# Attention groups in the order of dilation 1, 16, 4, loads in order of need, and the gate projection behind q

## What is computed

```python
ada = silu(c) @ w_ada + b_ada                      # shift, scale, gate: 3 x 1024
h = rms_norm(x, norm_g) * (1 + scale) + shift
z = h @ w_in                                       # 8704 columns
# branch A: three groups of 8 heads, each with its own q, k, v (512 columns each)
for g, (window, dilation) in enumerate(((128, 1), (512, 4), (2048, 16))):
    q = partial_rope(rms_norm(z_q[g])); k = partial_rope(rms_norm(z_k[g]))
    # a token attends to t - j * dilation, j = 0 .. 128, within its residue class
    o[g], denominator[g] = dilated_window_attention(q, k, z_v[g], window, dilation)
attn = sum of o[g], weighted by the softmax denominators over the groups
y_a = attn * silu(z_gate_a)
# branch B: chunked spatial gating
u, v = split(gelu(z_b)); v = layer_norm(v)
y_b = u * (tril(w_spatial) @ v + b_spatial) * silu(z_gate_b)
merged = sigmoid(z_mA) * (y_a @ w_branch_a) + sigmoid(z_mB) * (y_b @ w_branch_b)
out = x + gate * (merged @ w_out)
```

## Time and profile before

| | |
|---|---|
| median of 6 runs | 810.89 us (809.9 to 884.0) |
| the profiled execution, its own time | 810.75 us |
| span from its first to its last instruction, slowest core | 809.2 us |
| spans of the 8 cores | 805.3 to 809.2 us |
| PE busy | 741.5 us (92%) |
| DVE busy | 457.6 us (57%) |
| ACT busy | 375.4 us (46%) |
| POOL busy | 272.5 us (34%) |
| moved by DMA | 61.98 MB |

### The profile page before, as it was taken

One profiled execution on the slowest core, in us unless ns is written; L12 is line 12 of the kernel. 1 busy time (PEld: TensorE's weight loads), 2 busy tenths in 40 slices (PEclk: granted clock), 3 DMA queues, 4 the chain that ended last, 5 costly groups with the idle time before them and its releaser, 6 DMA issues.

```text
span 809.2 us, 14709 instructions; the slowest of 8 cores (805.3 to 809.2 us)
## 1 busy us (share of the span) xinstructions
PE 741.5 (92%) x4936; PEld 369.9 (46%) x4936; DVE 457.6 (57%) x730; ACT 375.4 (46%) x659; POOL 272.5 (34%) x332
## 2 busy tenths in 40 slices
PE   4776799999999899999888899989998999999996
PEld 0223455555666565454444444444443444444442
DVE  5335578876677577776666676566664222333333
ACT  2205678688766566676666655534221111111110
POOL 0002122433453434332122300367732333333334
PEclk9889899999999999999999999999999999999999
DMA  8992320360653000200000050709594122131314
GB/s 253 290 238 61 86 86 2 53 105 2 106 73 33 14 1 2 52 2 2 1 1 2 6 99 1 130 2 143 105 256 122 53 68 90 53 103 53 104 53 157
DMA packets 23481, 61.98 MB, mean 77 GB/s; under 512 B 5616, under 2 KB 12016, under 8 KB 20976
## 3 DMA queue, kind: packets, MB, share of 16 engines
q0 software_dynamic: 13472, 22.40, 18.2%
q1 hardware_dynamic: 7488, 30.26, 12.1%
q10 hardware_dynamic: 2448, 8.39, 2.6%
HBM read 75.05 MB, written 8.39 MB: 103 GB/s over the span
## 4 chain that ended last, share of the span: by engine, by line
PE 70%; DVE 9%; ACT 6%; issue 5%; DMA 4%; POOL 3%; SPq 1%; DVEq 0%; ACTq 0%; POOLq 0%
PE ps L236 61%; DVE arena L245 9%; ACT arena L245 6%; DMA arena<-w_ada 3%; POOL arena L245 3%; PE ps L368 2%; PE ps L548 2%; PE ps L581 2%; PE ps L508 2%; PE ps L585 1%; SPq L248 1%; PE ps L344 1%; PE ps L895 1%; DMA arena<-wsp 0%; DVEq L1043 0%
## 5 line engine op out<-in xcount | busy, mean ns | idle before, releaser
L236 PE MATMUL ps<-arena 128*128 128x512 bf16 x2692 | 615.7, 384 | 25.1 <-ACT arena L245 15.4
L236 PEld LDWEIGHTS ps<-arena 128*128 128x128 bf16 x2692 | 278.3, 108 | 315.8 <-issue 47.8
L245 POOL TENSOR_TENSOR arena<-arena 128x128 bf16<-128x128 f32 (+5 forms) x298 | 252.7, 856 | 441.7 <-DVE arena L245 421.5
L245 ACT ACTIVATE arena<-ps 128x1024 bf16<-128x1024 f32 (+2 forms) x283 | 193.9, 708 | 309.0 <-PE ps L236 216.2
L245 DVE TENSOR_TENSOR arena<-ps,arena 128x512 bf16<-128x512 f32 (+2 forms) x218 | 153.0, 734 | 90.7 <-ACT arena L245 41.3
L245 DVE SCALAR_TENSOR_TENSOR arena<-arena,ps 128x512 f32<-128x512 f32 x80 | 54.6, 686 | 119.9 <-PE ps L236 99.5
L245 DVE TENSOR_REDUCE arena<-arena 128x8 f32<-128x512 bf16 x96 | 65.8, 685 | 64.7 <-ACT arena L245 64.7
L245 ACT ACTIVATE arena<-arena 128x16 f32<-128x16 f32 (+5 forms) x185 | 77.9, 426 | 49.7 <-DVE arena L245 35.6
L245 DVE TENSOR_TENSOR arena<-arena 128x1024 bf16<-128x1024 bf16 (+5 forms) x116 | 72.5, 632 | 27.0 <-ACT arena L245 25.7
L245 ACT ACTIVATE arena<-ps,arena 128x512 bf16<-128x512 bf16 x96 | 60.9, 690 | 3.4 <-PE ps L508 3.4
L245 DVE TENSOR_SCALAR arena<-arena 128x256 bf16<-128x256 bf16 (+6 forms) x84 | 44.5, 571 | 24.7 <-ACT arena L245 17.6
(11 more groups left out here) (36 smaller groups left out, 134.8 us busy)
## 6 DMA issues: line engine op xcount, KB each, us to landing
arena<-x SPq DMA_DIRECT2D x32, 512.0 KB, 5.2
arena<-w_in POOLq DMA_DIRECT2D x16, 1024.0 KB, 14.6
out<-arena ACTq DMA_DIRECT2D x15, 512.0 KB, 4.9
arena<-w_ada SPq DMA_DIRECT2D x7, 1024.0 KB, 18.3
arena<-w_adag SPq DMA_DIRECT2D x8, 512.0 KB, 8.8
arena<-w_out POOLq DMA_DIRECT2D x2, 1024.0 KB, 29.2
arena<-w_ada SPq DMA_DIRECT2D x2, 512.0 KB, 32.9
arena<-w_in POOLq DMA_DIRECT2D x4, 256.0 KB, 9.0
```

Of the source, the lines that this page charges most:

```text
L236: ins = e.matmul(out_ap, l, r, start=(i == 0), stop=(i == n - 1))
L245: P.op(eng, lambda e: getattr(e, meth)(*a, **kw), reads=reads, writes=writes)
```

## The change

1. The groups come in the order of dilation 1, 16, 4. Each step of the first group needs one x tile of its own only, so names of scaled x (`hm`) are kept per tile, and x is scaled tile by tile and in pairs. The first group writes `acc`, now without a stride; the last, of dilation 4, adds.
2. SP loads w_ada 0, 1, 2, then x tiles 0 to 3, then w_ada 3; POOL loads Wq, Wk, Wv in halves, each gated by the landing of an earlier piece; x tiles 4 to 7 wait for Wv's first half.
3. At the start the rows, tables and x tiles come in another order; six of the eight scalings `x_mod4` stand in front of the last adaLN row. The x tiles 4 to 6 are prepared behind the q and k projections of steps 0 to 3 instead of between them.
4. `finZ` stands behind the next step's q projection, `finA` behind its k projection, `finB` behind its v projection; finB's product goes to POOL for token blocks 0 to 2.
5. The mask of the spatial weights is spread over 8 iterations.
6. `sv_mm` and `sv_y` come one step later for the first three token blocks, `gate_fin` and the outputs one merge later.

The diff, cut to its core:

```diff
+    def load_half(s, c0, h, gate):
+        P.op("pool", lambda e: e.dma_start(out=wslot[s][:, 4 * h:4 * h + 4, :], in_=win_v(c0, 512)[:, 4 * h:4 * h + 4, :]),
+             reads=[gate], writes=["ws%d" % s + "b" * h], slot="ws%d" % s + "b" * h)
...
         for c in range(4):
+            if c == 3:
+                for t in range(4):
+                    x_load(t)
...
-            if c < 2:
-                x_load(2 * c)
-                x_load(2 * c + 1)
-        dma("pool", wslot[0], win_v(1536, 512), "ws0", reads=["wada1_0"])
+        gate = "wada3_0"
+        for j in range(3):
+            for h_ in range(2):
+                load_half(j, 512 * j, h_, gate if h_ == 0 else "ws%d" % (j - 1) if j else "wada3_4")
+            gate = "ws%d" % j
...
-        dma("pool", wslot[1], win_v(2048, 512), "ws1", reads=["wada3_0"])
-        dma("pool", wslot[2], win_v(2560, 512), "ws2", reads=["wada3_6"])
...
-            x_load(t + 4, gate=["ws1"] if t >= 2 else [])
+            x_load(t + 4, gate=["ws2"])
         ada_row(0)
-        x_in(0, 3)
-        x_in(1, 4)
         ada_row(1)
         ada_col(0)
-        x_in(2, 5)
-        x_in(3, 6)
-        rot_tables(1)
+        rot_tables(0)
         ada_tr(0)
         ada_row(2)
         ada_col(1)
         rot_tables(2)
         ada_tr(1)
+        rot_tables(1)
+        for t in range(4):
+            x_in(t, 3 + t)
+        ada_col(2)
+        ada_tr(2)
+        for kc in range(6):
+            x_mod4(0, kc)
         ada_row(3)
-        ada_col(2)
-        rot_tables(0)
-        ada_tr(2)
         ada_col(3)
         ada_tr(3)
+        x_mod4(0, 6)
+        x_mod4(0, 7)
...
-        steps = [(1, r * 4 + n) for n in range(4) for r in range(4)]
+        steps = [(0, n) for n in range(16)]
         steps += [(2, r) for r in range(16)]
-        steps += [(0, n) for n in range(16)]
-        prev = [(s - 4 if s >= 4 else None) for s in range(16)] + [None] * 16 + [None] + list(range(32, 47))
+        steps += [(1, r * 4 + n) for n in range(4) for r in range(4)]
+        prev = [None] + list(range(15)) + [None] * 20 + list(range(32, 44))
...
-            X("dve", "tensor_tensor", [k0, k1], ["ya%d_%d" % (hp, tb), "ws4", "ws5"], out=y_aT[:, hp, ts_], in0=f0, in1=f1, op=ALU.mult)
+            X("dve" if tb == 3 else "pool", "tensor_tensor", [k0, k1], ["ya%d_%d" % (hp, tb), "ws4", "ws5"], out=y_aT[:, hp, ts_], in0=f0, in1=f1, op=ALU.mult)
...
             proj(it, 0)
             sumsq(it, 0)
+            if it - 1 in fin_at:
+                finZ(*fin_at[it - 1])
             if not one(b_):
                 scores(b_, 0)
                 mask(b_, 0)
-            if it - 1 in fin_at:
-                finA(*fin_at[it - 1])
-            if it + 5 < NT:
-                x_transp(it + 5, TB)
-                x_evac(it + 5, TB)
+            if it + 3 < NT:
+                x_transp(it + 3, TB)
+                x_evac(it + 3, TB)
...
             proj(it, 1)
             sumsq(it, 1)
             if it - 1 in fin_at:
-                finB(*fin_at[it - 1])
+                finA(*fin_at[it - 1])
...
-            if it in (4, 6, 8, 10):
-                x_mod(it + 4, 2)
+            if it in (4, 6, 8, 10, 12):
+                x_mod(it + 2, 2)
             proj(it, 2)
             vevac(it)
+            if it - 1 in fin_at:
+                finB(*fin_at[it - 1])
             transp(a)
-            if it in fin_at:
-                finZ(*fin_at[it])
...
-                for g_ in range(8):
-                    X("pool", "tensor_tensor", ["cst", "WsT"], ["WsT"], out=WsT[:, g_, :], in0=WsT[:, g_, :], in1=mD, op=ALU.mult)
+            if 25 <= it < 33:
+                X("pool", "tensor_tensor", ["cst", "WsT"], ["WsT"], out=WsT[:, it - 25, :], in0=WsT[:, it - 25, :], in1=mD, op=ALU.mult)
...
-            for n, ks in enumerate(((1, 2, 4, 5), (3, 5, 7, 8), (7, 9, 11, 12), (11, 13, 15, 15))):
+            for n, ks in enumerate(((1, 2, 5, 6), (3, 5, 8, 9), (7, 9, 12, 13), (11, 13, 15, 15))):
...
-                        gate_fin()
                         for t in range(4):
                             x2_load(t)
-                else:
-                    outp(8 * (tb - 1) + fc)
+                elif tb == 1:
+                    if fc == 0:
+                        gate_fin()
+                    else:
+                        outp(fc - 1)
+                        if fc == 7:
+                            outp(7)
+                elif tb == 2:
+                    outp(8 + fc)
+                elif fc > 0:
+                    outp(15 + fc)
+        outp(23)
```

More of the change, by code:

```diff
@@ L351, in x_mod4 @@
         def x_mod4(n, kc):
-            X("dve", "tensor_scalar", [B(3), B(4), B(5), B(6), "ab%d" % (kc // 2)], ["hm%d_%d" % (n, kc)],
+            X("dve", "tensor_scalar", [B(3), B(4), B(5), B(6), "ab%d" % (kc // 2)], ["hm%d_%d" % (4 * n + i_, kc) for i_ in range(4)],
               out=hT[:, kc, 0:512].rearrange("p (t w) -> p t w", t=4), in0=psb[:, 3:7, kc, :], scalar1=ab[:, 8 + kc:9 + kc],
@@ L358, in x_mod @@
                 dst = hT[:, kc, 128 * t:128 * (t + nt)]
-                X("dve", "tensor_scalar", ["hT%d" % i for i in range(t, t + nt)] + ["ab%d" % (kc // 2)], ["hm%d_%d" % (t // 4, kc)],
+                X("dve", "tensor_scalar", ["hT%d" % i for i in range(t, t + nt)] + ["ab%d" % (kc // 2)], ["hm%d_%d" % (i_, kc) for i_ in range(t, t + nt)],
                   out=dst, in0=dst, scalar1=ab[:, 8 + kc:9 + kc], scalar2=ab[:, kc:kc + 1], op0=ALU.mult, op1=ALU.add)
@@ L390, in fn @@
                 return ins
-            P.op("pe", fn, reads=["row%d" % br, "rowl%d" % br, "one11", "pT%d" % br], writes=[B(2)])
+            P.op("pe", fn, reads=["row%d" % br, "rowl%d" % br, "cst", "pT%d" % br], writes=[B(2)])
             cs = slice(2 * c, 2 * c + 2)
@@ L456, in proj @@
             w = wsl[g][role]
-            ns = [blk % 4] if g == 1 else range(4)
+            ns = [blk] if g == 0 else range(16)
             mm_group(banks[ZB(s, role)], [(hsl(g, blk, kc), wslot[w][:, kc, :]) for kc in range(KC)],
-                     reads=["ws%d" % w] + ["hm%d_%d" % (n, kc) for n in ns for kc in range(KC)], writes=[B(ZB(s, role))])
+                     reads=["ws%d" % w, "ws%db" % w] + ["hm%d_%d" % (n, kc) for n in ns for kc in range(KC)], writes=[B(ZB(s, role))])
         def sumsq(s, role):
@@ L528, in pt_new @@
         def pt_new(s, h):
-            i = pt_i[0] % (4 if s > 3 else 3)
-            pt_i[0] = i + 1
+            n = pt_i[0]
+            pt_i[0] = n + 1
+            i = n if n < 3 else (0, 3, 1, 2)[(n - 3) % 4]
             pt_of[(s, h)] = i
@@ L592, in accum @@
             dst, o = acc[:, h, :, tok_slice(g, blk)], banks[PB[h]].rearrange("p (m q) -> p m q", m=4)
-            if g == 1 and h == 1:
+            if g == 0 and h == 1:
                 X("act", "copy", [B(PB[h])], ["acc%d" % h], out=dst, in_=o)
-            elif g == 1:
+            elif g == 0:
                 X("dve", "tensor_copy", [B(PB[h])], ["acc%d" % h], out=dst, in_=o)
@@ L672, in build_nc @@
             rope(s)
-            if s == 3:
-                x_transp(6, TB)
-                x_evac(6, TB)
-            if s >= 2:
-                prep_own(4 + s)
-        for t in range(8, 12):
-            x_load(t, gate=["ws2"])
+        prep_own(4)
         proj(0, 2)
@@ L682, in build_nc @@
         transp(0)
+        prep_own(5)
         proj(1, 2)
         vevac(1)
-        x_transp(7, TB)
-        x_evac(7, TB)
-        x_mod(4, 4)
+        x_transp(4, XB)
+        x_evac(4, XB)
+        x_mod(4, 1)
         transp(1)
@@ L692, in build_nc @@
         mask(0, 0)
+        x_transp(5, XB)
+        x_evac(5, XB)
+        prep_own(6)
         transp(2)
-        prep_own(8)
-        prep_own(9)
         proj(3, 2)
         vevac(3)
-        x_transp(8, TB)
-        x_evac(8, TB)
-        prep_own(10)
-        for t in range(12, 15):
+        x_mod(5, 1)
+        prep_own(7)
+        x_transp(6, XB)
+        x_evac(6, XB)
+        for t in range(8, 12):
             x_load(t)
+        sc_x = x_prep(8, "dve", sx[:, 0:1], rx[:, 0:1], "sx0", "rx0", True)
         fin_at = {}
@@ L759, in build_nc @@
                 for j in range(3):
-                    load_w(j, 512 * j)
+                    load_w(j, 1536 + 512 * j)
             if it == 20:
@@ L772, in build_nc @@
                 load_w(1, OFF_GATE_B)
+        finZ(0, 2)
         scores(45, 0)
```

21 lines of the change are left out of this document (7 added, 14 removed).

## The result

The changed kernel takes 790.47 us (median of 10 runs, 789.93 at the lowest) against 811.16 us for the kernel before (20 runs): ratio 0.9745, 95% interval 0.9736 to 0.9754. The profiled execution took 789.74 us with a span of 788.2, so 1.5 us lie outside the span, as before. Some executions of either kernel (two of these ten) are slow ones, in which a die runs at a lower clock (a mean of 0.82 to 0.84 in these two): medians here count them, ratios leave them out. That it comes so close is partly luck: the misses of the terms, -5.4 and +4.6 us in all, cancel.

What follows compares the result with a forecast made beforehand. Bounds: loads at the start, then ACT, DVE and POOL chains, elsewhere PE at 93 to 100% except for named waits. Terms sum to -20.2 from 810.75 us, 790.55; with 0.14 about 790.7 us, range 779 to 802 (8 in 10).

Steps and rivals of the forecast that it cites:

- Loads and adaLN rows: Start up to the first q projection: new order of loads and rows gains 0 us, between -3 and +4.
- First q to the fourth step's q: Early projections without x tiles between them, Wq, Wk, Wv loaded by halves: -6.6 us, ends -11 and +4.2.
- rival B: Start gives nothing: each half load takes a whole load's 14.6 us, Wv lands at 84 us; 801.5 us, chance 0.20.
- x tiles in the loop: Loop steps 5 to 12: more steps carry x transposes and scalings, heavy steps 8.75 us; +1.3 us, ends -2 and +5.
- The mask: Spatial weights' mask spread over eight steps: PE's 2.04 us wait and 1.70 us of low clock go; -3.7 us.
- Dilation 4 last: Last attention group: four steps of one key block and one of two make it shorter; -2.1 us (-2.6 to -1).
- Gate projection: Branch A's gate projection moved behind q: step 10.94 to 10.35 us, eight times; -5.0 us, ends 0 and -12.7.
- Rival A: Gate projection flows freely, finA's product coming before v needs the bank: step 9.39 us, 783.0 us, chance 0.13.
- Rival E: Gate projection steps: DVE's mask slows beside POOL's longer work, some 0.6 us a step; 795.7 us, chance 0.06.
- Second half: Spatial products -0.9 us, wait before the gate's matmuls -2.3, last outputs -0.9: -4.1 us together.
- Rival C: Slower: more PE gaps between 73 and 91 us bring the low clock into loop steps; 813 us, chance 0.05.
- D: No change: the waits that go return elsewhere in full; 810.9 us, chance 0.03.

Runs made afterwards that it cites:

- control of group 3: The changed kernel, unaltered, run on the same chip as the third group's other runs: 790.84 us, ratio 0.975 to the kernel before.

## Why the prediction was right, point by point

- **Loads and adaLN rows**, predicted 0, measured -2.9, at the end of its range (-3 to +4). Mis-sized were rows 0 to 2: they ended at 31.25 us (24.22 + 7.03), not 33.1, since the first data came 1.1 us earlier than in the earlier trace rows, rows 0 and 1 took 15.52 us instead of 8.99 + 7.03, and the 0.5 us allowed between the rows was less. About a us of it is the choice of the core: over the eight cores of each trace q(0) starts at 53.8 to 56.9 us before and at 53.3 to 54.4 us after (52.8 to 56.1 in the later traces of the changed kernel), and the means, 55.7 and 53.9, differ by 1.8. The chain of the x transposes (9.6 us, counted as 10) and row 3's duration (9.55, counted as 9.93) were close. The term counted the loads as worth nothing, but only as a balance: with the old loads under the new program the same stretch ends at 65.5 us, 8.6 us later than before, so the order of the loads, worth 10.5 us there, pays for the new order of the rows.
- **First q to the fourth step's q**, predicted -6.6, measured -6.5 up to q(5). The path was the forecast's too: q(4) comes 34.6 us behind q(0) (91 - 57 = 34 in the forecast), and its square on ACT, which had no idle time before it, starts at 91.98 us, 37.9 us behind q(0) (94.6 - 57.0 = 37.6). The halves hid as reckoned; rival B (801.5, 0.20) is out, as a half took 6.8 us against the whole's 14.6.
- **x tiles in the loop**, predicted +1.3, measured +2.9. The failed step is "heavy steps 8.75 us": the step behind a scaling still took 9.19 us (q(5) to q(6), 97.92 to 107.11), as in the earlier trace rows. Four such steps miss by 1.8 us. The trace shows where the gain went. DVE works through such a step with one idle time, the 0.94 us for ACT that it had before too. The copy is shorter (0.68 us instead of 1.08), but the eight scalings behind it take 2.78 us instead of 2.47 for the same shape: they now start just behind an instruction of POOL's rotation, and the first alone took 0.72 us (rows under *DVE beside POOL* below). I ran nothing on it.
- **The mask**, predicted -3.7, measured -3.5 in its stretch. In the changed kernel's trace PE waits nowhere for POOL. The run with the block shows the sum of two parts of different kinds, 2.04 us of wait and 1.7 us of low clock, the second there on the slowest core of one trace and not of the other. Neither is there on every core: in the trace before, the wait was 2.0 to 2.3 us on five cores, with low clock behind it on each, and about 1.0 us on three, with none. Why the wait differs by core stays open.
- **Dilation 4 last**, predicted -2.1, measured -2.2. The order of the dilations alone was not run.
- **Gate projection**, predicted -5.0, measured -5.7; step 10.35 predicted, 10.19 measured, wait 0.9 and 0.89. The mechanism is shown by three runs: old place 10.95 us, product first 9.27, engine of the product without effect. Rival A (783.0) asked for the product before v needs the bank; the fixed order on DVE forbade it, and changing that order gave just this step. The 0.3 us that I allowed the product on POOL was wrong in place: nothing in the loop, 1.0 us at its end, where a short step wants the one buffer sooner. Of the tail's +2.2 us the runs explain 1.3; with all products on DVE, 0.9 us remains, of which 0.37 is a wait for DVE before the products with v.
- **Rival E** (DVE slows beside POOL, 795.7) is out: the mask that ran from 388.39 us took 0.68 us as in the earlier trace rows, with POOL's 4.03 us of work beginning 0.23 us after its start, and with the product on DVE the step was the same. But the prediction read the earlier trace rows wrongly as a row against contention: there and here the mask starts first, and it is POOL's instruction that takes longer, 0.98 us at 388.62 where the next of the same shape takes 0.67. The rule that I set against the row (the Trainium skill, GPSIMD Engine Reference, section 8) is borne out, below.
- **Second half**, branch B predicted -0.9, measured -0.3: of the second set's wait, "about 1.7 us" in the forecast, all 2.23 us stayed, because VectorE normalises between the halves of the sums (with the normalisations moved, 0.46 us). The third set still waits 0.63 us, where the forecast had nothing, and the fourth 0.99 instead of 0.34: 3.85 us in all, 3.80 before. Merges and outputs predicted -3.2, measured -4.9. The missing 1.7 us is the low clock behind the 2.31 us wait, which I had counted for the mask and not here; the run with the old outputs shows both parts.
- **Rival C** (the clock, 813) is out: the stretch from 57 to 98 us has 0.93 where it had 0.86, and the loop ran at 1.00. D fell with the result.

## What to carry to other kernels

When a wait for a bank moves rather than goes, look at what stands ahead of the releasing instruction in its own engine's queue: one swap of two instructions there took 0.93 us off the step (10.20 to 9.27), the whole move before it 0.75 (10.95 to 10.20). Price a wait on PE in two parts, its length and a chance of low clock behind it. And move an instruction off a busy engine only after a look at who waits for its result: here the busy engine was not the bound. Where DVE and POOL share a stretch, look at which of two instructions starts first: shortening one can make the next wait.

## What the runs showed of the hardware

**The same wait, two clocks.** A wait of 2.31 us was followed by a granted clock of 0.70 on core 6 and of 1.00 on core 0 of the same execution, in the windows above. The low level is 1.2 GHz, the other 2.4. The wait is certain, the low clock after it is not.

**A third level.** In all three groups cores of a die show a granted clock of 0.81 at times, neither of the two levels; the traces of the two kernels beside the result have none. A window of the control of group 3, core 0 and core 4:

```profile
576.00:578.00 2.00, 2.00 (x9) 0.87 (x8) 1.44 (x1) 0.60 (x1) 0.35 (x1) 0.81 1.01 242
...
576.00:578.00 2.00, 2.00 (x11) 0.89 (x10) 0.55 (x1) 0.72 (x2) 0.00 (x0) 1.00 1.07 251
```

The Trainium skill (TensorE: Matmul & The Clock Gate, Part 1) describes a limiter that takes a die to 13/16 of the clock when three of its cores run dense matmuls, and holds it while the load lasts. The level agrees (13/16 is 0.81); that it lasts as long as the load does not, in the executions traced: most of the dense stretches here, on all eight cores, ran at 1.00 (in the control of group 3 the loop, from 98 to 458 us, on every core); where 0.81 came, it was 13 to 39 us a core.

**DVE beside POOL.** In the changed kernel's branch B the same pair of normalisations (128x512, bf16 out of f32) took 0.97 us with POOL all but idle and 2.53 us beside POOL's products, which had started first:

```profile
509.27 0.97 DVE L249 TENSOR_SCALAR arena<-arena 128x512 bf16<-128x512 f32 x2
...
520.71 2.68 POOL L249 TENSOR_TENSOR arena<-arena 128x512 bf16<-128x512 f32 x2 [0.25 <-DVE arena L249]
...
521.14 2.53 DVE L249 TENSOR_SCALAR arena<-arena 128x512 bf16<-128x512 f32 x2
```

The scalings in the loop, of the same kind, first in the kernel before, then in the changed one (in each, the copy ahead of them and the eight scalings):

```profile
124.19 1.08 DVE L245 COPY arena<-ps 128x512 f32<-128x512 f32 x1
125.12 2.47 DVE L245 TENSOR_SCALAR arena<-arena 128x256 bf16<-128x256 bf16 x8
...
116.00 0.68 DVE L249 COPY arena<-ps 128x512 f32<-128x512 f32 x1
116.60 2.78 DVE L249 TENSOR_SCALAR arena<-arena 128x256 bf16<-128x256 bf16 x8
```

One that starts when POOL is between instructions takes 0.33 us. In the changed kernel the first starts 0.03 us after an instruction of POOL's rotation and takes 0.72 us; before, it started 0.36 us after one and took 0.39.

And an instruction with two SBUF inputs, the sum of the adaLN gate in the merges, twice beside POOL's product, which takes 1.27 us alone:

```profile
572.81 1.26 POOL L249 TENSOR_TENSOR arena<-arena 128x512 bf16<-128x512 f32 x1 [4.43 <-DVE arena L249]
572.89 2.26 DVE L249 SCALAR_TENSOR_TENSOR arena<-arena 128x1024 f32<-128x1024 f32 x1 [0.23 <-DMA arena<-w_adag]
...
576.27 1.27 DVE L249 SCALAR_TENSOR_TENSOR arena<-arena 128x1024 f32<-128x1024 f32 x1
576.49 2.18 POOL L249 TENSOR_TENSOR arena<-arena 128x512 bf16<-128x512 f32 x1 [2.42 <-DVE arena L249]
```

Where POOL started first, DVE's instruction took 2.26 us instead of 1.27; where DVE did, POOL's took 2.18. The Trainium skill (GPSIMD Engine Reference, section 8) names two kinds of VectorE instruction that contend with GpSimd: those in a mode that uses two ports, and those with two SBUF inputs. These rows bear it out for the second kind, and show that the one that starts second pays. The normalisations and scalings have one tensor input each; that they are of the first kind fits, but the trace doesn't say which mode they ran in.
